# A fused RWKV / GLA / MoE layer on one core: the first RWKV half step moved in among the taps of the last convolution

## The reference, cut to what matters

```
rkv = short_conv(cat[r, k, v], rw_conv, grid)   # 3x3 depthwise over the latent grid, 3 taps over context
kk  = normalised(k * rw_k_k)                    # per head
for d in (forward, backward):
    w = exp(-0.606531 * sigmoid(...)); a = sigmoid(...); kd = k * (1 + (a - 1) * rw_k_a)
    S_t = S_{t-1} (diag(w_t) + a_t^T b_t) + v_t^T k_t      # a_t = -kk, b_t = kk * a
    y_t = S_t r_t
bonus = sum(r * k * rw_r_k) * v
```

## Time and profile before

| | us |
|---|---|
| median of 3 runs | 982.75 |
| lowest and highest of the 3 | 978.35 and 985.03 |
| the profiled execution | 982.82 |
| its span, first to last instruction | 981.0 |
| TensorE busy in it | 873.4 (89%) |
| VectorE busy | 560.7 (57%) |
| ScalarE busy | 334.1 (34%) |
| GpSimd busy | 146.8 (15%) |

### The profile page before, as it was taken

One profiled execution on the slowest core, in us unless ns is written; L12 is line 12 of the kernel. 1 busy time (PEld: TensorE's weight loads), 2 busy tenths in 40 slices (PEclk: granted clock), 3 DMA queues, 4 the chain that ended last, 5 costly groups with the idle time before them and its releaser, 6 DMA issues.

```text
span 981.0 us, 21494 instructions
## 1 busy us (share of the span) xinstructions
PE 873.4 (89%) x8900; PEld 535.9 (55%) x8900; DVE 560.7 (57%) x933; ACT 334.1 (34%) x585; POOL 146.8 (15%) x296
## 2 busy tenths in 40 slices
PE   2799999999999988778888987899994799999996
PEld 0445445655555544567777776745574354444442
DVE  1524016689967798756556664697326145554467
ACT  3222111133023758376556653312210122232223
POOL 6000101112000011334232231000001001000041
PEclk9899999999899989799999999999985799999998
DMA  9810433014224400211212211591009589999957
GB/s 330 325 64 1 134 131 102 22 69 150 87 86 172 172 1 11 40 30 31 41 32 38 49 33 49 177 363 44 33 11 342 193 276 369 369 370 368 340 125 228
DMA packets 119760, 142.46 MB, mean 145 GB/s; under 512 B 49964, under 2 KB 85224, under 8 KB 119272
## 3 DMA queue, kind: packets, MB, share of 16 engines
q1 hardware_dynamic: 110824, 116.55, 36.2%
q0 software_dynamic: 3744, 13.63, 4.5%
q10 hardware_dynamic: 5088, 10.82, 2.9%
HBM read 122.99 MB, written 18.00 MB: 144 GB/s over the span
## 4 chain that ended last, share of the span: by engine, by line
PE 78%; DVE 12%; issue 4%; ACT 3%; DMA 2%; SPq 1%; ACTq 0%; DVEq 0%; POOLq 0%
PE bank L1947 70%; PE bank L1951 8%; DVE rk_r L1406 2%; DMA region<-in_w_ada_dram 2%; ACT region L933 1%; DMA rk_r<-h_rows_dram,slot_tokens 1%; DVE region L1406 1%; DVE rk_r L1407 1%; DVE cl_b L1319 1%; DVE cl_b L1865 1%; DVE region L1936 0%; ACT w_sb L933 0%; DVE region L1350 0%; DVE region L1932 0%; ACT ada_row_buffers L933 0%
## 5 line engine op out<-in xcount | busy, mean ns | idle before, releaser
L1947 PE MATMUL bank<-region 64*64 64x64 f32 (+3 forms) x3904 | 400.6, 299 | 16.1 <-issue 7.1
L1947 PEld LDWEIGHTS bank<-region 64*64 64x64 f32 (+1 forms) x3904 | 232.5, 149 | 170.0 <-issue 159.2
L933 ACT ACTIVATE region<-bank 128x256 f32<-128x256 f32 (+3 forms) x216 | 98.1, 454 | 352.0 <-PE bank L1947 256.6
L1951 PE MATMUL bank<-ident,region 128*128 128x128 f32 (+2 forms) x403 | 67.3, 301 | 27.7 <-DMA scratch<-in_gla_gk_dram 12.6
L1947 PE MATMUL bank<-region,rk_r 128*128 128x512 f32 x176 | 80.3, 610 | 0.8 <-issue 0.8
L1951 PEld LDWEIGHTS bank<-ident,region 128*128 128x128 f32 (+2 forms) x403 | 49.6, 154 | 43.9 <-issue 34.3
L1917 DVE TENSOR_SCALAR region<-region 128x256 f32<-128x256 f32 x16 | 4.7, 294 | 100.6 <-ACT region L933 100.6
L1406 DVE SCALAR_TENSOR_TENSOR rk_r<-region,vec,rk_r 128x512 f32<-128x512 f32 x64 | 50.3, 786 | 12.3 <-ACT rk_r L933 10.2
L1947 PEld LDWEIGHTS bank<-region,rk_r 128*128 128x128 f32 x176 | 33.7, 196 | 39.7 <-issue 38.6
L908 POOL DMA_INDIRECT rk_r<-h_rows_dram,slot_tokens x16 | 15.2, 952 | 245.6 <-PE bank L1951 132.0
L1588 DVE TENSOR_TENSOR region<-bank,region 128x256 f32<-128x256 f32 x60 | 25.5, 425 | 41.5 <-PE bank L1947 40.2
(11 more groups left out here) (277 smaller groups left out, 1151.9 us busy)
## 6 DMA issues: line engine op xcount, KB each, us to landing
region<-in_moe_w_dram SPq DMA_DIRECT2D x38, 1024.0 KB, 10.3
region<-in_w_ada_dram SPq DMA_DIRECT2D x12, 2048.0 KB, 8.7
region<-in_w_in_dram SPq DMA_DIRECT2D x6, 2048.0 KB, 7.8
cl_b<-in_moe_w_dram SPq DMA_DIRECT2D x10, 1024.0 KB, 12.7
expert_rows_dram<-yg_b ACTq DMA_DIRECT2D x14, 512.0 KB, 6.8
region<-late_condition_dram SPq DMA_DIRECT2D x3, 1024.0 KB, 9.7
a_rows_dram<-region SPq DMA_DIRECT2D x20, 128.0 KB, 2.9
region<-inverse_rows_dram SPq DMA_DIRECT2D x20, 128.0 KB, 3.0
```

The costliest lines, as they stand in the source:

```text
L933: return act.activation(out, in_, func, **kw)
L1947: return pe.matmul(out, lhsT, rhs, start=start, stop=stop)
L1951: return pe.transpose(out, in_, ident[0:n, 0:n])
```

## The change

TensorE makes the bonus product between the units v2 and v3 instead of behind v3. The front half of step 0 (pass -1) is taken out of the loop, which now begins at H = 0, and written out by hand on every engine: on TensorE it starts right behind v3 and stops ahead of the wait for the convolutions at X32; behind that wait only tile 0 of v is transposed and used at once, and the other four tiles follow behind Z32, ahead of L 2 and X64. VectorE puts `r_and_k(0)`, `a_and_b(1)` and the masks of step 0 ahead of v3's taps, X16's addition in the middle of the taps and X32's behind them; the convolution is split in `taps` and `line_taps` for it. `r_and_k(1)`, which stood ahead of X64's addition, now stands behind it. GpSimd inverts the blocks of step 1 ahead of `b_product(2)` and `k_product(1)`. The list of banks follows. SP's code is the same. Every computation is the same as before, in another order.

```diff
--- before.py
+++ after.py
@@ -342,8 +342,7 @@
         jobs += unit("k0") + [("ada", 8)] + unit("k1") + turn(8) + [("ada", 9)] + rank_jobs("w", 0)
         jobs += unit("k2") + turn(9) + [("ada", 10)] + rank_jobs("a", 0) + unit("k3") + turn(10) + [("ada", 11)] + rank_jobs("w", 1)
         jobs += unit("v0") + turn(11) + rank_jobs("a", 1) + [("kl", i) for i in range(RC)] + [("kc",)]
-        jobs += unit("v1") + [("L", 0, 0), ("L", 0, 1)] + unit("v2") + unit("v3") + [("bonus",), ("L", 1, 0), ("L", 1, 1)]
-        jobs += [("vt", t) for t in range(NT)]
+        jobs += unit("v1") + [("L", 0, 0), ("L", 0, 1)] + unit("v2") + [("bonus",)] + unit("v3")
         NS = 2 * NT
 
 
@@ -351,7 +350,10 @@
             return [key + (0,), key + (1,)]
         ORD = [0, 3, 2, 4, 1]
         fill = {"X64": [("gate", 0)], "G": [("yT", 0, 0), ("yT", 0, 1)]}
-        for H in range(-1, NS):
+        jobs += pair("k", 0) + pair("L", 1) + [("tK", 0)] + pair("b", 0) + pair("Z8", 0) + [("X8t", 0), ("tB", 0), ("tA", 0)]
+        jobs += pair("X16", 0) + pair("Z16", 0) + [("X16t", 0)] + pair("X32", 0) + [("vt", 0), ("AV", 0), ("X32t", 0)] + pair("Z32", 0)
+        jobs += [("vt", t) for t in range(1, NT)] + pair("L", 2) + pair("X64", 0)
+        for H in range(NS):
             s, l = H + 1, H + 3
             inside = lambda h, js: js if 0 <= h < NS else []
             last = lambda h, key: fill[key] if h == NS - 1 else []
@@ -880,7 +882,10 @@
             k_product(0)
             inverse_of_eights(0)
             b_product(1)
-            for H in range(-1, NS):
+            inverse_of_eights(1)
+            b_product(2)
+            k_product(1)
+            for H in range(NS):
                 if H + 3 < NS:
                     b_product(H + 3)
                 if 0 <= H + 2 < NS:
@@ -1207,13 +1212,29 @@
             act.wait_ge(s_cl, 2)
             decays(1)
             raw_input("v3")
+            growths_for_k(0)
             growths_for_b(1)
             first_taps("v3")
-            growths_for_k(0)
             raw_blocks(1)
-            for t in range(NT):
+            turned("tK", 0)
+            k_factors(1)
+            by_chunk("Z8", 0)
+            turned_x("X8t", 0)
+            turned("tB", 0)
+            decays(2)
+            growths_for_b(2)
+            turned("tA", 0)
+            by_chunk("Z16", 0)
+            turned_x("X16t", 0)
+            copy_out(vtok[:, 0], ("vt", 0))
+            scored_v(0)
+            turned_x("X32t", 0)
+            by_chunk("Z32", 0)
+            for t in range(1, NT):
                 copy_out(vtok[:, t], ("vt", t))
-            for H in range(-1, NS):
+            growths_for_k(1)
+            raw_blocks(2)
+            for H in range(NS):
                 s, o, l = H + 1, H + 2, H + 3
                 back, new, next_, later = H >= 0, 0 <= s < NS, 0 <= o < NS, l < NS
                 if next_:
@@ -1398,14 +1419,21 @@
                     chunk_sums(gcl[:, d, i], d)
 
 
-            def conv(n):
+            def taps(n, a, b):
                 c_, dst, lat, line, out = conv_views(n)
                 dve.wait_ge(s_tap, c_ + 1)
-                for m in range(1, 9):
+                for m in range(a, b):
                     i, j = m // 3, m % 3
                     own(STT(out, lat[:, i:i + GH, j:j + GW], tap(c_, i, j), out, ALU.mult, ALU.add))
+
+            def line_taps(n):
+                c_, dst, lat, line, out = conv_views(n)
                 own(STT(dst[:, 0:P], line[:, 1:P + 1], tap(c_, 1, 1), dst[:, 0:P], ALU.mult, ALU.add))
                 tell(STT(dst[:, 0:P], line[:, 2:P + 2], tap(c_, 1, 2), dst[:, 0:P], ALU.mult, ALU.add), s_conv)
+
+            def conv(n):
+                taps(n, 1, 9)
+                line_taps(n)
 
             def og_bounded(t):
                 wait_filled(dve, "og", t)
@@ -1729,15 +1757,25 @@
             for i in range(RC):
                 tell(STT(prod[:, i], rT[:, i], vec[:, vrk + i:vrk + i + 1], kT[:, i], ALU.mult, ALU.mult), s_bon)
             conv("v2")
-            wait_filled(dve, "pc", "v3")
-            a_and_b(1)
-            conv("v3")
+            tell(dve.memset(MR[:, 0], 0.0), s_mst)
             wait_filled(dve, "bonus")
             out_of(dve.tensor_copy(bonus[:, :], bank(("bonus",))[:, 0:NT * NH]), "bonus")
-            tell(dve.memset(MR[:, 0], 0.0), s_mst)
+            wait_filled(dve, "pc", "v3")
             r_and_k(0)
+            a_and_b(1)
+            masked_a(0)
+            masked_k(0)
+            masked_b(0)
+            taps("v3", 1, 5)
+            grown("X16", 0)
+            taps("v3", 5, 9)
+            line_taps("v3")
+            grown("X32", 0)
+            a_and_b(2)
+            grown("X64", 0)
             wait_filled(dve, "vt", NT - 1)
-            for H in range(-1, NS):
+            r_and_k(1)
+            for H in range(NS):
                 s, o, l = H + 1, H + 2, H + 3
                 back, new, next_, later = H >= 0, 0 <= s < NS, 0 <= o < NS, l < NS
                 if new:
@@ -2467,23 +2505,44 @@
             project("v1", w, P)
             scores("L", 0)
             project("v2", w, 2 * P)
-            project("v3", w, 3 * P)
             pe.wait_ge(s_bon, RC)
             b = open_bank("bonus")
             for t in range(NT):
                 for i in range(RC):
                     ins = mm(b[:, t * NH + 2 * i:t * NH + 2 * i + 2], prod[:, i, t * P:(t + 1) * P], blk[:, 0:P:HD])
             finish(ins)
-            scores("L", 1)
-            pe.wait_ge(s_conv, 3 * RC)
-            for t in range(NT):
+            project("v3", w, 3 * P)
+            def turned_v(t):
                 b = open_bank("vt", t)
                 for i in range(RC):
                     ins = tr(b[:, i * P:(i + 1) * P], vT[:, i, t * P:(t + 1) * P])
                 finish(ins)
-            for t in range(NT):
+
+            scores("k", 0)
+            scores("L", 1)
+            turned("tK", 0)
+            scores("b", 0)
+            times_u("Z8", 0)
+            turned_x("X8t", 0)
+            turned("tB", 0)
+            turned("tA", 0)
+            grown("X16", 0)
+            times_u("Z16", 0)
+            turned_x("X16t", 0)
+            grown("X32", 0)
+            pe.wait_ge(s_conv, 3 * RC)
+            turned_v(0)
+            wait_result(pe, "vt", 0)
+            scored_v(0)
+            turned_x("X32t", 0)
+            times_u("Z32", 0)
+            for t in range(1, NT):
+                turned_v(t)
+            scores("L", 2)
+            grown("X64", 0)
+            for t in range(1, NT):
                 wait_result(pe, "vt", t)
-            for H in range(-1, NS):
+            for H in range(NS):
                 s, l = H + 1, H + 3
                 back, new, later = H >= 0, 0 <= s < NS, l < NS
                 if new:
```

## The result

The change costs time: the kernel takes 985.92 us (median of 20 runs) against 979.79 for the kernel before (20 runs), a ratio of 1.0063 with the interval 1.0042 to 1.0084, so +6.1 us by the medians and +6.2 by the ratio. One of the 20 runs of the changed kernel took 1317 us at a granted clock of 0.64, and the ratio leaves it out. The forecast was +4.0 on a profiled execution of 982.8, with 980.0 to 992.0 as its range.

A forecast was written before the change was run, and what follows sets the result against it. The prediction took TensorE's chain, with its hole before v3's convolution ends, as the bound. A 4.2 us later WU of step 0, -1.3 for the early inverse and 1.1 for low clock gave 982.8 + 4.0 = 986.8 us, range 980.0 to 992.0.

The forecast's parts named there:

- the hole of 6 us: TensorE idles 6.08 us ahead of v's transposes, waiting for v3's convolution; the front half of step 0 could fill it.
- a shift goes through from WU0 on: From the start of WU of step 0 (433.18) TensorE is nearly always busy, so a shift there reaches the end.
- Part 1: Bonus between v2 and v3: starts at 392.2, clock falls, v3 ends at 408.6, VectorE idles some 7 us.
- Rival A: The clock holds in the bonus and behind the convolution: 979.7 us, faster than before; chance 0.15.
- Part 2: VectorE from v3's end to the convolution's end: 15.3 us of work plus 1.0 of stalls, ending at 425.0.
- rival C: ScalarE's `k_factors(1)` holds up X16, perhaps X32, so VectorE stands 2 us among the taps: 988.8 us; chance 0.15.
- Part 3: From the convolution's end to WU of step 0: starts at 437.4 against 433.18, 4.2 us later.
- Part 4: Inverse 1 early on GpSimd, done at about 427.2: the 1.32 us idling ahead of Z8 of step 1 goes, -1.3.
- rival B: GpSimd's small instructions keep the taps' rhythm, blocks land 2 us later, L 2 starts 2.3 late: 989.1 us; chance 0.10.
- The sum: Whole kernel: 4.2 - 1.3 = 2.9, plus 1.1 for a low clock stretch, +4.0, giving 986.8 us; chance 0.50.
- one more low stretch in pass 0: An extra low-clock stretch of some 2 us in pass 0, costing 1.1 us, bounds 0 and 1.7.
- rival D: Clock low through the whole bonus and most of the thin stretch behind it: 990.8 us; chance 0.10.

The follow-up runs named there:

- the third experiment: The changed kernel with each of the 40 bonus matmuls moving 128 columns instead of 2: 984.44 us, 1.0056 of the kernel before.
- The second experiment: The kernel before with only the bonus product moved ahead of v3: 988.39 us, 1.0099 of the kernel before.
- the first: The changed kernel with the bonus product back behind v3: 977.44 us, 0.9983 of the kernel before.
- the fourth: The changed kernel with `r_and_k(1)` ahead of X64's addition on VectorE: 983.24 us, 1.0033 of the kernel before.
- the fifth: The changed kernel with GpSimd's order as before, `b_product(2)` and `k_product(1)` ahead of inverse 1: 989.26 us, 1.0089 of the kernel before.
- the sixth experiment: The kernel before with only GpSimd's order changed, inverse 1 ahead of `b_product(2)` and `k_product(1)`: 979.98 us, 0.9991 of the kernel before.
- the short chain: Seventh kernel: the changed one with bonus behind v3, GpSimd's old order, v's transposes ahead of AV, WU ahead of k of step 1: 976.89 us, 0.9965 of before.
- eighth: The short chain with GpSimd's inverse 1 ahead of `b_product(2)` and `k_product(1)`: 974.05 us, 0.9931 of the kernel before.

## Why the prediction was right, and where its sum was off

**The place of the change** was right: the hole of 6 us is on the chain. That a shift goes through from WU0 on was right only roughly: the change is 5.8 us late at WU0, 4.2 at G0 and 5.5 at k2. Over the nine changed kernels of the table the time follows k2 (the difference of the ratio from 1, times 980 us): +5.5 at k2 goes with +6.2 us, +7.4 with +9.7, -5.8 with -6.8, and the two kernels within 0.5 of before at k2 are those whose interval holds 1. It doesn't follow it to the microsecond (+6.6 goes with +8.7, -4.8 with -3.4), and the profiled pair shows why I don't read further: the shift of after against before, 5.5 at k2, has shrunk to 1.2 by the state products of the tenth half step, in an execution that is 2.6 below its median, beside one of before that is 3.0 above its own. Where the 0.6 us between 5.5 at k2 and the 6.1 of the medians lie stays open.

**Part 1** was right in mechanism and in size. On before's clock the bonus product starts at 392.1 (forecast 392.2), v3 ends at 408.9 (408.6), and VectorE idles 7.65 us ("some 7"). The split was off a little: the product took 1.1 us longer and not 1.5, v3 2.4 (against the third experiment) to 2.9 (against 8.4) and not 2.0. The clock is the smaller part of this bill; the product's own time ahead of v3 is the larger, and the third experiment leaves it in place. The second experiment shows the cost alone, the first takes it away, the third shows which part of it is the clock. Rival A, that the clock holds, needed the product to run without a fall, and it fell in all four kernels that have it ahead of v3 with 2 columns (the change, the second, the fourth and the fifth). Its sum also let the stalls of 1.0 us go with the clock, without a reason: in the third experiment the clock is up, and the small copy beside `b_product(1)` still takes 1.15.

**Part 2** was right: from the start of `r_and_k(0)` (408.13) to the end of the convolution (424.55) 16.4 us, forecast 15.3 + 1.0. Of the two stalls that I had named only the first came, the collision with `b_product(1)`: the small copy of 0.17 us takes 1.15 beside it (408.85 and 408.19). X16 and X32 were added directly behind the taps (419.73 and 424.59), so rival C did not occur. The Trainium skill, page "SBUF — State Buffer", section "Who interferes with whom", has that rule: a plain VectorE copy can take both port pairs and then shuts GpSimd out or is shut out; the 1.15 agrees.

**Part 3** was right up to Z32 and too small behind it. AV starts 1.49 us behind the convolution (forecast 1.6) and takes 1.97 (1.96). Z32 is done at 430.11. Then the four transposes of v, L 2 and X64, for which I had written 3.3, end at 433.51 + 0.69 = 434.20, 4.1 later, of which the transposes have 3.02 and not 2.0: the clock is low until 432. From AV's start to X64's end it is 8.16 us instead of 7.0. k of step 1 starts at 438.1 on before's clock, forecast 436.25. This is the term that was mis-sized, by 1.8 us: 0.28 were there at AV's start, 1.16 came from there to X64, and 0.37 in the addition and `r_and_k(1)`. I had priced AV at the low level because the trace of before showed it so, and let the four transposes behind it run at full clock without a reason. The 3.03 us of waiting ahead of k of step 1 was seen and is `r_and_k(1)`, but only 1.1 of it is the order of VectorE's queue.

**Part 4** had the right event and the wrong credit. The idle time ahead of Z8 went, in the change and in the sixth experiment, and in the latter the credit is 1.4 us at G0. But 1.0 of it is gone at k2, where the "issue" gap has appeared, so the -1.3 of the sum was worth some -0.4 there; the change has a gap of 1.31 in the same place. That the one brings the other is not shown: in the fifth experiment the wait ahead of Z8 is gone too, and there is no gap. The blocks landed 2.9 us later than forecast (421.45, or 422.3, against 419.4), as rival B had it, and the inverse was done 1.1 later (428.3 against 427.2), since ten of the 14 instructions took 0.2 to 0.3, and only four 0.5 or more. The products behind it were late by 2.78 us for VectorE and early enough for TensorE; rival B's price was wrong, its event was right.

**The sum**: +4.2 at WU0, less 1.3 of credit, plus 1.1 for one more low stretch in pass 0, made +4.0. Measured at the marks: +5.8 at WU0 (some 439.0 on before's clock, against 433.18), +4.2 at G0, +5.5 at k2. The extra low stretch of pass 0 did not come: the clock is at 1.00 from 434 to 480 in the trace of after, and it is the trace of before that has a low stretch at 472 to 478. So the 1.1 stood for something that did not happen, and that the sum of 4.0 lies so near the 4.2 of G0 is luck: it about makes up for what part 3 lacked. What came in pass 0 was the gap of 1.31 us, and it was in no term. Of rival D, a low clock for most of the thin stretch, the windows show the half.

## What to carry to other kernels

A product of many matmuls with two columns can cost more than its own length where a dense group stands behind it, here 2.4 to 2.9 us in v3: measure its place by what the next group takes too. Before moving work into a hole, name which engine opens the hole and whether anything moved ahead of that point holds it back: here 5.6 us of TensorE's work ahead of v3 held VectorE up for 7. And when two engines hold each other up, put the long instructions where the critical engine pauses and the short ones beside its work: the order of GpSimd's queue alone was worth 1.0 us at the first state product in the short chain, and 1.5 us at the convolution's end.

## What the runs showed of the hardware that was not expected

- **The clock and two columns.** 40 matmuls of 2 columns in a row let the granted clock fall from 1.00 to 0.50 though TensorE had no pause in them, within the product in all four kernels that have it ahead of v3, and between some 0.5 us ahead of its end and 1.0 behind it in the five that have it behind v3; the same 40 with 128 columns, with the same 0.41 us of idling ahead of them, left it at 1.00, in one trace. The price ahead of v3: 1.1 us in the product and 2.4 to 2.9 in v3 (in the fourth experiment 1.6, and 1.9 to 2.3). The fall was expected as likely; that the columns and not the count or the weight loads decide it was not.
- **A low stretch moves.** k of step 1 and WU0, 64 matmuls, take 2.85 us in the change and 4.45 in the fifth experiment, where they start only 0.8 us later (58.39 against 57.60). It cost 1.6 to 1.7 us in three of the experiments, the first, the third and the fifth. A gain at one mark of a thin stretch can't be added to a gain at the next.
- **Long GpSimd products hold taps up, short instructions don't.** Two products of 1.3 to 1.6 us stretched four taps from 3.12 to 4.90 us in the short chain and to 4.01 in the fifth experiment; beside the 14 small instructions the four taps kept 3.12, and the small ones took 0.71 instead of 0.24. The rule of the page "SBUF — State Buffer" of the Trainium skill, cited in the prediction, says that the two shut each other out; what each pays depends on which is long.
- **A gap without a wait.** In seven of the ten kernels TensorE stops for 0.76 to 1.51 us at the v products of step 0, 6.2 to 7.0 us behind G0, with "issue" as the profile's reason and no wait on a semaphore: 1.31 in the change, 1.51, 0.76, 1.31, 1.03, 1.31 and 1.31 in the first, third, fourth, sixth, seventh and eighth kernels, and none in the kernel before, the second or the fifth. The second still has its idle time ahead of Z8, as the kernel before has. The fifth has not, and its k of step 1 and WU0 are at the low clock, but so are those of the first and the third, which have the gap. A supply of instructions that is late when TensorE runs without a pause would look like this, but packets of the instruction queue are in the traces of both kinds, and no run was made that separates it. It stays open.
